# First four outputs behind each layer norm computed from the raw sums, scaled afterwards

## The reference

```python
def _layer_norm(x, g, b):
    xf = x.astype(F32)
    mu = jnp.mean(xf, -1, keepdims=True)
    var = jnp.mean(jnp.square(xf - mu), -1, keepdims=True)
    return ((xf - mu) * lax.rsqrt(var + LN_EPS) * g + b).astype(x.dtype)
...
x = _layer_norm(DEEPNORM_ALPHA * x + (1 + ga1) * y, ln_g[i, 0], ln_b[i, 0])
u = x * (1 + sc2) + sh2
gate, up = jnp.split(u @ ffn_w_in[i], 2, axis=-1)
y = (jax.nn.silu(gate) * up) @ ffn_w_out[i]
x = _layer_norm(DEEPNORM_ALPHA * x + (1 + ga2) * y, ln_g[i, 1], ln_b[i, 1])
```

## Time and profile before

| | |
|---|---|
| median of 3 runs | 2300.97 us (2295.56 to 2305.91) |
| the profiled execution | 2309.86 us |
| its span, first to last instruction | 2308.0 us |
| PE matmul busy | 2120.9 us (92% of the span) |
| PEld weight loads busy | 1923.8 us (83%) |
| DVE busy | 1211.5 us (52%) |
| ACT busy | 869.0 us (38%) |
| POOL busy | 707.0 us (31%) |
| chain that ended last, by engine | PE 80%, DVE 12%, ACT 3% |

### The profile page before, as it was taken

The page is one execution under the profiler, slowest core; times in us unless marked ns, Lnnn a source line. Parts: engine busy times, 40 slices in busy tenths (PEclk is TensorE's granted clock), DMA queues, the critical chain, the costliest instruction groups (busy, mean ns, idle before and its releaser), DMA issues.

```text
span 2308.0 us, 40812 instructions
## 1 busy us (share of the span) xinstructions
PE 2120.9 (92%) x17730; PEld 1923.8 (83%) x17730; DVE 1211.5 (52%) x2208; ACT 869.0 (38%) x1258; POOL 707.0 (31%) x316
## 2 busy tenths in 40 slices
PE   3989997999889988999999889899999998988997
PEld 3867875889889887898999885699989997857897
DVE  6156444764582446653642656554265428457652
ACT  0442111444353223543433443343343334434543
POOL 0340001314674003126314550131461165304124
PEclk9998998999999989999999998899999999989999
DMA  8564442455434003554445340244434543303552
GB/s 327 226 270 148 149 149 74 146 183 186 157 132 147 2 2 128 186 196 166 162 168 183 128 147 19 91 165 167 181 134 176 175 173 110 128 19 146 184 191 83
DMA packets 49682, 340.44 MB, mean 148 GB/s; under 512 B 6368, under 2 KB 8416, under 8 KB 8672
## 3 DMA queue, kind: packets, MB, share of 16 engines
q1 hardware_dynamic: 49504, 337.84, 40.5%
HBM read 336.77 MB, written 1.05 MB: 146 GB/s over the span
## 4 chain that ended last, share of the span: by engine, by line
PE 80%; DVE 12%; ACT 3%; issue 2%; DMA 2%; POOL 1%; SPq 0%; ACTq 0%; POOLq 0%; DVEq 0%
PE bank L532 80%; DMA ada_ring<-ada 2%; POOL ring_low L2516 1%; DVE arena L1899 1%; DVE arena L1884 1%; ACT high L1471 1%; DVE small L1894 1%; PE bank L538 1%; DVE arena L1927 1%; DVE arena_parts L1922 1%; DVE arena L1914 0%; DVE ZZ L2108 0%; DVE arena L2096 0%; DVE small L2482 0%; DVE small L2371 0%
## 5 line engine op out<-in xcount | busy, mean ns | idle before, releaser
L532 PE MATMUL bank<-arena_parts,high 128*128 128x272 f32 (+2 forms) x4512 | 1028.0, 315 | 63.6 <-ACT arena_parts L1496 38.0
L532 PEld LDWEIGHTS bank<-arena_parts,high 128*128 128x128 f32 x4512 | 751.6, 192 | 114.0 <-issue 52.1
L532 PE MATMUL bank<-arena_parts,ring_low 128*128 128x272 f32 (+2 forms) x2736 | 782.9, 289 | 0.0
L1471 ACT ACTIVATE high<-ring 128x2048 fp32r<-128x2048 f32 x237 | 453.1, 1914 | 681.0 <-PE bank L532 597.1
L2516 POOL TENSOR_TENSOR ring_low<-ring,high 128x2048 fp32r<-128x2048 f32 x105 | 489.7, 4666 | 690.4 <-ACT high L1471 690.3
L532 PEld LDWEIGHTS bank<-arena_parts,ring_low 128*128 128x128 f32 (+1 forms) x2736 | 524.3, 192 | 0.9
L1935 DVE TENSOR_TENSOR ring_low<-ring,high 128x2048 fp32r<-128x2048 f32 x132 | 318.7, 2415 | 185.6 <-ACT high L1471 185.6
L532 PE MATMUL bank<-hidden_high,high 128*128 128x256 f32 (+1 forms) x1056 | 303.2, 287 | 0.0
L532 PE MATMUL bank<-hidden_low,high 128*128 128x256 f32 (+1 forms) x1056 | 301.1, 285 | 0.0
L532 PE MATMUL bank<-hidden_high,ring_low 128*128 128x256 f32 (+1 forms) x1056 | 300.1, 284 | 0.0
L2516 POOL TENSOR_TENSOR hidden_low<-arena,hidden_high 128x256 fp32r<-128x256 f32 (+1 forms) x132 | 105.6, 802 | 586.1 <-DVE hidden_high L1951 585.9
(11 more groups left out here) (330 smaller groups left out, 2272.5 us busy)
## 6 DMA issues: line engine op xcount, KB each, us to landing
ring<-stream SPq DMA_DIRECT2D x269, 1024.0 KB, 4.8
ada_ring<-ada SPq DMA_DIRECT2D x48, 1024.0 KB, 5.6
con<-consts SPq DMA_DIRECT2D x1, 1542.5 KB, 11.5
con<-consts SPq DMA_DIRECT2D x1, 1040.0 KB, 7.1
arena<-xin SPq DMA_DIRECT2D x1, 1024.0 KB, 11.8
out<-arena SPq DMA_DIRECT2D x2, 512.0 KB, 2.9
prob_even<-consts SPq DMA_DIRECT2D x1, 320.0 KB, 11.8
par<-params SPq DMA_DIRECT2D x1, 272.5 KB, 9.7
```

The source lines that it names most:

```text
L532: ins = nc.tensor.matmul(o, l, r, start=start, stop=stop_, skip_group_check=True)
L1471: act(high[:, q % HIGHS], ring[:, s % RING], ACT.Copy).then_inc(a.sig(high_ready), 1)
```

## The change

It opens eight of the nine stages (all but that of norm 3) with `raw_four` in the place of `first_four`. The residual less the provisional mean, times the gain, is split into a high and a low part before the mean and the variance are known; the four output tiles are computed from these, with four more columns of gains and biases behind the tokens; afterwards VectorE adds the gain column times the shift of the mean, multiplies by the reciprocal deviation (both in the bank), and the bias column comes in with the next operation or as another term (`scale_opened`). The inputs of the rest of the stage are made later: ScalarE writes high part and whole tile, two operations each, and VectorE's whole tiles fall away. VectorE takes slab 2's rest over from GpSimd, ahead of the normed tiles; `residual_base` moves behind output f = 1 or behind the third convolution. TensorE makes a second provisional mean in bank 6 for the eighth tile.

```diff
 def low_by_vector_engine(q):
-    return STAGES[n] == "ffn" and HIGHS <= q - STAGE_AT[n] < HIGHS + FT
+    at = q - STAGE_AT[n]
+    return at == HIGHS - 1 or STAGES[n] == "ffn" and HIGHS <= at < HIGHS + FT
...
# TensorE
                 mm(bank[4][:, 0:T], cm("mean"), x_sums(1, T), False, False)
+                mm(bank[6][:, 0:T], cm("half_mean"), x_sums(0, T), True, True, hold=True).then_inc(full["vector"][6], 1)
+            def raw_four(n, tiles, T, signals):
+                for b in range(4):
+                    eng.wait_ge(*freed(b))
+                eng.wait_ge(square_added, pe.nth(square_added, 6))
+                eng.wait_ge(raw_high_ready, pe.nth(raw_high_ready, 1))
+                eng.wait_ge(raw_low_ready, pe.nth(raw_low_ready, 1))
+                for k in range(DT):
+                    eng.wait_ge(raw_high_ready, pe.nth(raw_high_ready))
+                    eng.wait_ge(raw_low_ready, pe.nth(raw_low_ready))
+                    blocks = [split_block((*tile, k)) for tile in tiles]
+                    both, low = raw_both(n, k, T), raw_low(n, k, T)
+                    if k == DT - 1:
+                        for b, (w_high, w_low) in enumerate(blocks):
+                            m = mm(bank[b][:, 0:T], w_high, low, False, False, hold=b == 3)
+                        m.then_inc(opened, 1)
+                    for b, (w_high, w_low) in enumerate(blocks):
+                        if k == 0 and b == 2:
+                            mean_sum(T)
+                        mm(bank[b][:, 0:T + 4], w_high, both, k == 0, False)
+                        m = mm(bank[b][:, 0:T + 4], w_low, both, False, k == DT - 1, hold=k == DT - 1)
+                        if k == DT - 1:
+                            m.then_inc(signals[b], 1)
+                    if k == 0:
+                        square_sum(T)
+                    if k < DT - 1:
+                        for b, (w_high, w_low) in enumerate(blocks):
+                            m = mm(bank[b][:, 0:T], w_high, low, False, False, hold=b == 3)
+                        m.then_inc(opened, 1)
+            def normal_tile():
+                eng.wait_ge(input_high_ready, pe.nth(input_high_ready))
+                eng.wait_ge(input_low, pe.nth(input_low))
...
# ScalarE
+            def raw_tile(n, j, T):
+                act(raw_high(n, j, T), tl(9, j, T), ACT.Copy, scale=lnc[:, n, 0, j:j + 1]).then_inc(a.sig(raw_high_ready), 1)
-            def norm_out(n, T, signal=input_high_ready):
+            def norm_out(n, T):
+                weights_high(STAGE_AT[n] + 2)
                 for j in range(DT):
                     eng.wait_ge(normed, a.nth(normed))
+                    if raw:
+                        eng.wait_ge(opened, done + max(min(j + 2, DT - 1), j + 1))
+                    for to, signal in ((input_high(STAGES[n], j, T), input_high_ready), (tl(US, j, T, xview(T)), whole_ready)):
+                        act(to, tl(9, j, T), ACT.Identity, bias=lnc[:, n, 1, j:j + 1],
+                            scale=lnc[:, n, 0, j:j + 1]).then_inc(a.sig(signal), 1)
+                weights_high(STAGE_AT[n] + HIGHS)
...
# VectorE
+            def raw_rest(n, js, T):
+                    nv.scalar_tensor_tensor(out=raw_low(n, j, T), in0=tl(9, j, T), scalar=lnc[:, n, 0, j:j + 1],
+                                            in1=raw_high(n, j, T).bitcast(F32), op0=ALU.mult,
+                                            op1=ALU.subtract).then_inc(v.sig(raw_low_ready), 1)
...
                 centers = [center(0)]
+                eng.wait_ge(std_ready, v.nth(std_ready))
+                nv.reciprocal(small[:, 2, 0:T], small[:, 1, 0:T]).then_inc(v.sig(vstep), 1)
+                centers += [center(1), center(2), center(3)]
+                if n < len(STAGES):
+                    weights_low(STAGE_AT[n] + 2)
+            def scale_opened(b, T, signal, to_bias):
+                both = bank[b][:, T:T + 4].rearrange("p (a e) -> p a e", e=2)
+                nv.tensor_reduce(opening_cols[:, b], both, AX_X, ALU.add).then_inc(v.sig(vstep), 1)
                 eng.wait_ge(*v.last)
+                product = bank[b][:, 0:T]
+                for i in range(1 if to_bias else 2):
+                    nv.scalar_tensor_tensor(out=product, in0=small[:, i, 0:T], scalar=opening_cols[:, b, i:i + 1], in1=product,
+                                            op0=ALU.mult, op1=ALU.add).then_inc(v.sig(vstep), 1)
+                    eng.wait_ge(*v.last)
+                nv.tensor_tensor(product, product, small[:, 2, 0:T], ALU.mult).then_inc(v.sig(signal), 1)
...
# VectorE, ffn
+                    if f < 2 and raw:
+                        eng.wait_ge(gate_full, full_gate + f + 1)
+                        scale_opened(2 * f, T, gate_scaled, True)
+                        eng.wait_ge(up_full, v.nth(up_full))
+                        scale_opened(2 * f + 1, T, vstep, True)
...
+                        gate_halves(f, T)
+                        if f == 0:
+                            weights_low(q0 + HIGHS)
+                        weights_low(q0 + HIGHS + 1 + f)
+                        if f == 1:
+                            residual_base(n, T)
+                        continue
...
# VectorE, convolve, and the loop in the mixer
+                if n < 4:
+                    scale_opened(b, T, vstep, False)
+                    eng.wait_ge(*v.last)
...
+                    if n == 2:
+                        residual_base(4 + 3 * l, T)
...
# GpSimd
                 eng.wait_ge(input_low, g.nth(input_low, DT))
-                weights_low(q0 + 2)
+                if STAGES[n] != "ffn":
+                    weights_low(q0 + HIGHS)
                 base_sums(To)
```

316 lines of the change are left out of this document (193 added, 123 removed).

## The result

The changed kernel takes 2319.0 us (median; 2317.5 to 2326.0), the kernel before 2301.0 (2295.6 to 2305.9): a ratio of 1.0088, 95% interval 1.0070 to 1.0106. The prediction was 2325 in a range of 2297 to 2346. TensorE's busy time did not move (2121.6 us); VectorE has 40 us more work (1251.7) and ScalarE 60 more (928.8), GpSimd 44 less (663.3). What moved on TensorE are its waits.

The account below looks back on a forecast made before the run. TensorE bounds the kernel (80% of the chain of waits). FFN 0.8, norm 3 3.6, mixers 13.4, delta net 3.3, second mean 2.4, last norm 0.6 sum to +24 us on the median 2300.97: 2325, range 2297 to 2346.

Parts of the forecast that it names:

- The list at the norm: From VectorE taking up the last result tile (T0): slab 2's rest ends T0+9.9, ScalarE's last low part is written T0+18.9.
- f = 3 and f = 5: FFN outputs at norm 0: f = 3 starts T0+25.1, f = 5 T0+37.5; FFN stages together +0.8 us.
- the clock: FFN stages: TensorE idling brings the lower clock, half a loss of 2.4 us at each of two places, +6.0 us.
- Norm 3: Norm not opened raw but given the new list: TensorE starts at T0+10.0 instead of 6.3, +3.6 us.
- The mixers: Norms 4 and 7: scalings and base delay TensorE's bank 0 to T0+41.0 instead of 35.3; +6.7 us each, +13.4.
- The delta net: Norm 1: convolution 6, ahead of TensorE's wait for bank 2, ends between T0+54 and 56.5; +3.3 us.
- The second mean and the last norm: Second provisional mean in TensorE's way, 0.24 us ten times, +2.4; two more centerings at the last norm, 0.6.
- The rival's drain: FFN stages: drain with ScalarE's table load, f = 3 1.4 us later, up to 7 us more over five stages.
- (a): Eight norms: TensorE's gap goes and nothing comes for it, -57 us, 2244; chance 0.03.
- (b): FFN stages keep their gain, -23 us, 2301, chance 0.2; with the mixers' wait also hidden 2288, 0.1 more.
- (c): GpSimd's base sums and slab collide with VectorE's critical stretch in eight stages, +38 us, 2360; chance 0.1.
- (d): TensorE stays at the lower clock through f = 3 and f = 4 in five stages, +6 us, 2331; chance 0.15.

Follow-up runs that it names:

- experiment 1: Changed kernel with VectorE taking slab 2's rest behind the fourth normed tile (at norm 3 behind the last low part): 2301.9 us, ratio to before 1.0019.
- experiment 7: Changed kernel, ScalarE writing no whole tiles, VectorE making low parts from the normed tile without the norm's bias (result off, time only): 2300.1 us.
- the repeat of before: The kernel before, unchanged, run and profiled once more: 2299.2 us, span 2297.1.
- experiment 3: Changed kernel without the twelve scalings of opened products in delta net and mixers (time only): 2303.2 us.
- experiment 9: Experiment 8 with only FFN stages opened, softplus rows behind convolution 23, base behind convolution 2, slab 4 ahead of GpSimd's base sums in mixers and delta net: 2280.2 us.
- experiment 2: Changed kernel with slab 2's rest back on GpSimd, early, ahead of its wait for the low inputs: 2319.05 us.
- experiment 8: Experiment 1 with slab 3's rest taken ahead of hidden tile 0 in the FFNs: 2288.65 us.
- experiment 5: Experiment 1 with only the five FFN stages opened raw; delta net and mixers unscaled, base ahead of convolutions, unopened norms in the order of before: 2300.0 us.
- experiment 10: Experiment 9 with no raw opening at all: 2296.1 us, ratio to before 0.9987.
- experiment 11: Experiment 9, mixers reordered: base, memset, small operation ahead of convolution 0, decay operations behind silu 5, GpSimd's base sums ahead of slab 3: 2257.6 us.
- experiment 6: Experiment 1 with the mixers' base, small and decay operations behind convolution 5 or silu 5, delta net's softplus rows behind convolution 23: 2306.3 us.

## Why the prediction was right, point by point

The sum said +24, the measurement is +18.0 by medians, of which the traces put 17.1 into the stages. Of the 7 us between 24.1 and 17.1 the delta net has 4 and the FFN stages 2. By its steps:

- **The list at the norm**: right. It had slab 2 end at T0+9.9 and the last low part at 18.9; the trace has the first normed tile start at 9.9 and the last low part end at 18.9 (429.79 with its 0.43). Experiments 1 and 7 show that both causes it named, the slab's place and ScalarE's two operations a tile, hold TensorE.
- **f = 3 and f = 5**: f = 3 was put at T0+25.1 and came at 25.2, f = 5 at 37.5 and came at 37.3. The FFN sum was +0.8 and 1.2 for the mean products; measured +0.1 against the repeat of before and -4.6 against the first profile. The term that was too large is the clock, +6.0. The lower stretch did come, 428.4 to 435.0 at 0.50, but at norm 0 it lay on work in front of a wait: f = 2 ended 2.5 us later than put, and the idleness of 3.0 us became 0.6. At norms 5 and 6, where -2.1 each was put from the rows of the first profile, the trace has -3.2 and -1.7 against that profile and -1.0 and -0.9 against the repeat.
- **Norm 3**: +3.6, measured +3.5.
- **The mixers**: +13.4, measured +13.8 against the repeat of before, +11.6 against the first profile. The wait was to end at T0+41.0 and ends at 40.8 in both, so the step holds. That the sum fits to 0.4 us is luck: one by one the mixers are +12.4 and +1.4 against the repeat, +6.6 and +4.9 against the first profile, where +6.7 each was put, and the clock makes the difference. The scalings were put at 7.1; left out in experiment 3, the wait ended 6.5 earlier. In the sum stands, unnamed, that GpSimd's slab no longer holds an operation ahead of the convolutions, about 4 us in the kernel before (experiment 9): the sum started the convolutions at the last low input, and without that credit the loss would have been larger.
- **The delta net**: +3.3, measured -0.7: the one step whose sign is off. The wait was put at T0+54 to 56.5 and ends at 55.4, after a first one of 4.8 us until T0+38.8 that the prediction doesn't have; so the step holds. What did not come is the loss at the stage's end, and I had not looked at the clock in the chunk part; in experiment 2, with the lower stretch there as in both traces of before, the stage is +3.4. That two traces differ in it is shown, and that 3.3 was the price without the luck of the clock is argued from this one pair; why the stretch is there or not is open.
- **The second mean and the last norm**: 0.24 ten times and 0.6; the last stage measures +0.5. The 2.4 of the others are inside the stages, and no run takes them apart.
- **The rival's drain**: the Trainium skill (ScalarE: Activation LUTs, What ACT_TABLE_LOAD costs) adds a drain of about 1.4 us to a table load. At norm 0 of the changed kernel ScalarE's timeline decides it:

```profile
429.59 1.89 ACT L1574 ACTIVATE high<-ring 128x2048 fp32r<-128x2048 f32 x1
431.50 1.28 ACT L1631 ACT_TABLE_LOAD   x1
432.80 0.47 ACT L1631 ACTIVATE silu_t<-bank,opening_cols 128x256 f32<-128x256 f32 x1
```

The bank was scaled at 431.27, so nothing held silu 0 but the load, and it stands 0.02 behind the operation ahead and 0.02 ahead of silu: 1.32 in all from one operation to the next. The sum by 1.28 was the right one.

Rivals: (a) fell: it asked for ScalarE's last high part before T0+12.3, which begins at T0+17.3 at norm 0. (b) fell as the change was written; with the order of two slabs mended, as in experiments 1 and 8, the FFN stages gain 14.9 us of its 23. (c) did not come as a rule, but once on the path: in the delta net of the changed kernel an operation of 8x256 (651.95) took 3.28 us where 0.41 is usual, until the end of GpSimd's slab at 654.95, ahead of the wait for bank 2. The prediction had it, as what is left of the 5.8 us. More came in experiments 2, 5, 9 and 10, where a slab or a base had been moved. (d) came as a stretch, at a cost of 0 us at norm 0 and 0.6 at norm 2.

## What to carry to other kernels

Work that starts earlier gains only what the step behind it lets through: with a gap filled on the engine that bounds the kernel, look at once at the list of the engine that feeds it, operation by operation, for what stands ahead of the first thing waited for and is itself needed later (here a slab of 2.2 us, whose place cost some 17). Of a moved operation, follow every in-order queue that waits for its signal: the base behind convolution 5 cost GpSimd's slabs their time. Where an opening adds operations on the feeding engine ahead of a bank's release, as the scalings do in the mixers, it loses, as experiment 3 shows for the order of the changed kernel; opened mixers in the order of experiment 11 were not run. Where the additions fall into that engine's slack, as in the FFNs, it pays.

## What the runs showed of the hardware

- VectorE's tiny operation with two SBUF operands (12x1) stood 3.65 us beside GpSimd's slab, 0.15 to 0.20 without it: the collision cost what was left of GpSimd's instruction, not what the size of VectorE's would suggest. The eight base scalings, with one SBUF tile each, were held too (7.04 for 2.75). The centerings with a bank as an operand (1.82 for three, experiment 2) and the convolution steps that read a bank (1.57 for three beside the slab at 1334.68 of the changed kernel) were not.
- A low stretch of the clock is worth what stands behind it: 6.6 us at 0.50 cost nothing ahead of a wait, and 5.6 us at 0.70 ate 0.7 of 1.8 us won. At f = 3 of the FFN stages at T = 256 gaps of 2.8 us were followed by it in experiments 1, 5 and 6, gaps of 1.6 us in experiments 8, 9 and 11 were not; at T = 272 the same gap of 2.6 us was followed by it in experiments 5 and 6 and not in experiment 1.
- A reduction of four columns in a bank takes 0.15 us, with the next start 0.19 behind it (0.2 was assumed).
